# Moving key and value projections and attention heads to other places of a two-layer mixer block

## The reference, cut to what matters

```python
mem_n = rms_norm(mem, mem_norm_g)
for l in range(2):
    h = rms_norm(x, pre_mix_g[l])
    proj = h @ w_in[l]            # lx, ly, fq, fk, fv, ff, rq, rk, rv, rg
    lru_out = rg_lru(conv(lx)) * gelu(ly)                 # recurrence over time
    fox_out = forgetting_attention(fq, fk, fv, ff, b_f)   # 8 heads, causal, forget gate ff
    ret_out = retention(rq, rk, rv, rg, positions)        # 4 heads, rotary, decay
    x = x + rms_norm(concat(lru_out, fox_out, ret_out) @ w_out[l], post_mix_g[l])
    h = rms_norm(x, pre_cross_g[l])
    k, v = mem_n @ w_ck[l], mem_n @ w_cv[l]               # depend on mem only, not on x
    x = x + rms_norm(attend(h @ w_cq[l], k, v) @ w_co[l], post_cross_g[l])
    h = rms_norm(x, pre_ffn_g[l])
    x = x + rms_norm((silu(h @ w_gate[l]) * (h @ w_up[l])) @ w_down[l], post_ffn_g[l])
```

## Time and profile before

| | |
|---|---|
| Median of 3 runs | 2499.45 us (2499.06 to 2500.43) |
| The profiled execution | 2499.28 us, span 2497.5 us |
| PE busy | 1922.5 us (77%), 12804 instructions |
| DVE busy | 812.4 us (33%) |
| ACT busy | 520.6 us (21%) |
| POOL busy | 82.9 us (3%) |
| DMA | 739.81 MB, mean 296 GB/s |

### The profile page before, as it was taken

The page is one execution under the profiler, slowest core; times in us unless marked ns, Lnnn a source line. Parts: engine busy times, 40 slices in busy tenths (PEclk is TensorE's granted clock), DMA queues, the critical chain, the costliest instruction groups (busy, mean ns, idle before and its releaser), DMA issues.

```text
span 2497.5 us, 29128 instructions
## 1 busy us (share of the span) xinstructions
PE 1922.5 (77%) x12804; PEld 1253.0 (50%) x12804; DVE 812.4 (33%) x1271; ACT 520.6 (21%) x776; POOL 82.9 (3%) x140
## 2 busy tenths in 40 slices
PE   8999899979998999788766666666666566665665
PEld 7769799869797999677411221121221122111221
DVE  4545467666454576655301100110001010110012
ACT  5434433335254333333100000000000000000000
POOL 1100000011000000010000000000000000000000
PEclk9869999989799999887788877877877778786887
DMA  8215366744153667534799999999999999999996
GB/s 266 99 59 178 105 205 221 237 156 152 60 179 102 205 224 245 169 102 168 293 429 430 429 429 428 429 429 429 429 429 430 429 428 430 428 431 428 430 428 277
DMA packets 171069, 739.81 MB, mean 296 GB/s; under 512 B 6672, under 2 KB 133136, under 8 KB 146240
## 3 DMA queue, kind: packets, MB, share of 16 engines
q1 hardware_dynamic: 168592, 731.27, 73.5%
q0 software_dynamic: 2352, 6.69, 0.8%
HBM read 736.88 MB, written 1.05 MB: 295 GB/s over the span
## 4 chain that ended last, share of the span: by engine, by line
DMA 50%; PE 33%; DVE 11%; ACT 4%; issue 2%; SPq 0%; POOL 0%; DVEq 0%; ACTq 0%
PE PS L317 32%; DMA WB<-in_w_down 23%; DMA WB<-in_w_up 22%; DMA W<-in_w_down 5%; DVE WL L1354 4%; DVE S L1349 3%; ACT WH L911 2%; DVE X L1349 1%; DVE N L1419 0%; PE PS L499 0%; DMA W<-in_w_in 0%; DVE C L1346 0%; DVE S L1346 0%; DVE T L1346 0%; POOL T L2022 0%
## 5 line engine op out<-in xcount | busy, mean ns | idle before, releaser
L317 PE MATMUL PS<-WB,XS 128*32 128x352 f32 x3072 | 364.9, 637 | 210.6 <-DMA WB<-in_w_up 123.8
L1354 DVE TENSOR_TENSOR WL<-W,WH 128x2048 fp32r<-128x2048 f32 x141 | 325.1, 2305 | 245.7 <-ACT WH L911 245.6
L317 PE MATMUL PS<-WB,S 128*32 128x512 f32 x1408 | 273.5, 769 | 150.4 <-issue 77.7
L317 PEld LDWEIGHTS PS<-WB,XS 128*32 128x32 f32 x3072 | 116.6, 141 | 456.7 <-issue 179.4
L317 PE MATMUL PS<-HTh,WH 128*128 128x256 f32 x1064 | 307.5, 289 | 10.1 <-DVE WL L1354 4.7
L911 ACT ACTIVATE WH<-W 128x2048 fp32r<-128x2048 f32 x141 | 269.0, 1908 | 207.6 <-DMA W<-in_w_down 106.2
L1349 DVE SCALAR_TENSOR_TENSOR S<-S,PS 128x352 f32<-128x352 f32 (+1 forms) x110 | 63.3, 587 | 759.9 <-ACT S L1319 752.6
L317 PE MATMUL PS<-HTl,WH 128*128 128x256 f32 x1064 | 302.9, 285 | 0.0
L317 PE MATMUL PS<-HTh,WL 128*128 128x256 f32 x1064 | 302.7, 284 | 0.0
L317 PEld LDWEIGHTS PS<-WB,S 128*32 128x32 f32 x1408 | 73.3, 128 | 339.8 <-issue 225.4
L317 PEld LDWEIGHTS PS<-HTh,WH 128*128 128x128 f32 x1064 | 205.9, 194 | 12.7 <-DVE WL L1354 5.2
(11 more groups left out here) (262 smaller groups left out, 2188.8 us busy)
## 6 DMA issues: line engine op xcount, KB each, us to landing
WB<-in_w_down SPq DMA_DIRECT2D x64, 2816.0 KB, 36.0
WB<-in_w_gate SPq DMA_DIRECT2D x48, 2816.0 KB, 35.7
WB<-in_w_up SPq DMA_DIRECT2D x48, 2816.0 KB, 35.6
C<-in_w_gate SPq DMA_DIRECT2D x16, 2816.0 KB, 36.1
C<-in_w_up SPq DMA_DIRECT2D x16, 2816.0 KB, 37.3
W<-in_w_in SPq DMA_DIRECT2D x31, 1024.0 KB, 7.5
S<-in_w_ada SPq DMA_DIRECT2D x24, 1024.0 KB, 5.3
W<-in_w_gate SPq DMA_DIRECT2D x22, 1024.0 KB, 10.0
```

What stands on the lines that cost most here:

```text
L317: return e.matmul(o, l, r, start=start, stop=stop, skip_group_check=True)
L1354: e.tensor_tensor(M.WL[i][:, :], M.W[:, 2048 * (m % NW):2048 * (m % NW) + 2048], M.WH[i][:, :].bitcast(F32), ALU.subtract).then_inc(*up("l ...
```

## The change

One table, `FILL`, says where each of the 16 key and value units of both layers goes. In each mixer three of them stand among the heads and the output units; the others stand after the post-norms, by `norm_after`, in three programs (PE's is shown). Layer 1's keys are made after layer 0's cross attention and feed-forward. In the mixer attention heads start after the fifth unit and one stands between each pair of units; the output units of the attention come before that of the recurrence, between retention heads. On DVE a head's maxima come before the next unit's low half and its probabilities after it; on ACT a head's exponents come after the high half. `Beside` gets a second lane, in which the parameters and the memory's norm advance at the same time as the forget gate and the recurrence. In the feed-forward the modulation load comes after the down unit's, and the first one of a layer waits for the mixer's output product and not for the cross attention's. `CV` and `CK` get the columns of `XN` and `GA`, `post_norm` works in the first 2048 columns of `S`, the accumulators `AD` move to free columns of `C1`, and the gate bias is loaded in layer 1's feed-forward. The cross attention's first query unit waits for each part of its input as it needs it.

```diff
+FILL = {("mix", 0): (("k", 0), ("k", 1), ("k", 2)), ("post_mix", 0): (("k", 3), ("v", 0), ("v", 1), ("v", 2), ("v", 3)),
+        ("post_cross", 0): (("k", 0), ("k", 1)), ("post_ffn", 0): (("k", 2), ("k", 3)),
+        ("mix", 1): (("v", 0), ("v", 1), ("v", 2)), ("post_mix", 1): (("v", 3),), ("post_cross", 1): (), ("post_ffn", 1): ()}
...
-        self.jobs = []
-
-    def add(self, *jobs):
-        self.jobs.extend(jobs)
+        self.lanes = [[], []]
+
+    def add(self, *jobs, lane=0):
+        self.lanes[lane].extend(jobs)
 
     def step(self, n=1):
         for _ in range(n):
-            if self.jobs:
-                try:
-                    next(self.jobs[0])
-                except StopIteration:
-                    self.jobs.pop(0)
+            for jobs in self.lanes:
+                if jobs:
+                    try:
+                        next(jobs[0])
+                    except StopIteration:
+                        jobs.pop(0)
 
     def finish(self, job):
-        while job in self.jobs:
+        while any(job in jobs for jobs in self.lanes):
...
-    M.CST = C1[:, 0:NCONST]
+    M.CST, M.AD = C1[:, 0:NCONST], [C1[:, NCONST + 256 * i:NCONST + 256 + 256 * i] for i in range(2)]
...
-    M.CQ, M.CK, M.CV = view(0, 8, 256), view(2048, 8, 256), view(4096, 2, 1024)
+    M.CQ, M.TMP = view(0, 8, 256), view(0, 2, 1024)
+    M.CV, M.CK = M.XN, N1[:, 2048:4096].rearrange("p (a b) -> p a b", a=8)
     M.A = [view(512 * i, 2, 256) for i in range(2)]
-    M.AD = [view(1024 + 256 * i, 256) for i in range(2)]
...
+    def norm_after(place, name, layer):
+        units = FILL[place]
+        nrm = norming(name)
+        next(nrm)
+        if len(units) < 2:
+            for u in units:
+                fill(layer, *u)
+            for _ in nrm:
+                pass
+            return
+        for u in units[:-1]:
+            fill(layer, *u)
+        beside.add(nrm)
+        fill(layer, *units[-1])
+        beside.finish(nrm)
...
+        heads(0)
+        proj_t("w_in", l, 3, HT, ("q", l, 1))
+        heads(1)
+        proj_t("w_in", l, 5, HT, ("kk", l, 1))
+        heads(2)
+        proj_r("w_in", l, 7, HT, ("vv", l, 1))
+        heads(3)
+        proj_r("w_in", l, 8, HT, ("rq", l), off=8)
+        heads(4)
+        proj_r("w_in", l, 9, HT, ("rk", l), off=8)
+        heads(5)
+        proj_r("w_in", l, 10, HT, ("rv", l), off=8)
+        heads(6)
+        proj_r("w_in", l, 11, HT, ("rg", l), off=8)
+        heads(7)
+        if l == 0:
+            beside.finish(memory)
+            e.wait_ge(*free("turn", ("mem",), 6))
+        f0, f1, f2 = FILL[("mix", l)]
+        fill(l, *f0)
+        heads(8)
+        e.wait_ge(*at("rot", l, 1, 1))
+        for w, src in (("tq", M.RQ), ("tk", M.RK)):
+            for _ in turning((w, l), [src[:, 0, :], src[:, 1, :]], 2):
+                pass
+        fill(l, *f1)
+        heads(9)
+        ret_s(0)
+        ret_s(1)
+        y = ("mix", l)
+        e.wait_ge(*free("o", l, 1))
+        out_unit("w_out", l, 1, y, of=None if l == 0 else ("ffn", l - 1), start=True)
+        beside.finish(rec)
+        psY = two(take(("ry", l), hold=True))
+        ret_v(0)
+        ret_v(1)
+        ret_s(2)
+        ret_s(3)
+        e.wait_ge(*free("o", l, 3))
+        out_unit("w_out", l, 2, y)
+        ret_v(2)
+        ret_v(3)
+        drop(("ry", l))
         last = retained()
         beside.add(last)
         e.wait_ge(*at("lru", l))
-        y = ("mix", l)
-        out_unit("w_out", l, 0, y, of=None if l == 0 else ("ffn", l - 1), start=True)
-        e.wait_ge(*free("o", l, 3))
-        out_unit("w_out", l, 1, y)
-        out_unit("w_out", l, 2, y)
+        out_unit("w_out", l, 0, y)
+        fill(l, *f2)
         beside.finish(last)
         e.wait_ge(*free("turn", ("ret", l), 0))
         out_unit("w_out", l, 3, y, last=True)
...
             proj_t("w_up", l, n, HT, ("u", l, n))
-            C.units.order.append(("ada", 12 * l + n))
             if n > 1:
                 down(n - 2)
+            C.units.order.append(("ada", 12 * l + n))
         down(9)
-        C.units.order.append(("ada", 12 * l + 11))
         ada_sum(12 * l + 9)
         down(10)
+        C.units.order.append(("ada", 12 * l + 11))
...
+    pre_norm(("mix", 0))
     for l in range(2):
-        pre_norm(("mix", l))
         mixer(l)
-        e.wait_ge(*free("turn", ("mem",), 6))
-        fill_k(l, 0)
-        nrm = norming(("cross", l))
-        fill_k(l, 1)
-        next(nrm)
-        fill_k(l, 2)
-        beside.add(nrm)
-        fill_k(l, 3)
-        for n in range(4):
-            fill_v(l, n)
-        beside.finish(nrm)
-        e.wait_ge(*free("turn", ("cross", l), 6))
+        norm_after(("post_mix", l), ("cross", l), l)
         cross(l)
-        pre_norm(("ffn", l))
+        norm_after(("post_cross", l), ("ffn", l), 1)
         ffn(l)
+        if l == 0:
+            norm_after(("post_ffn", 0), ("mix", 1), 1)
...
+        unit(heads, 0)
+        q_out(1)
+        unit(heads, 1)
...
         def heads(i):
             if i < 8:
-                scores(i)
+                maxima(i)
+            unit(rest, i)
+        def rest(i):
+            if i < 8:
+                probabilities(i)
...
+        heads(8)
+        heads(9)
+        decayed(0)
+        decayed(1)
+        beside.finish(rec)
+        decayed(2)
+        decayed(3)
...
+        if l:
+            e.wait_ge(*at("y", "cross", 1))
+            for g in range(2):
+                e.dma_start(M.GA[:, g, :], D["b_ada_2"][0:1, 2048 + 3072 * g:3072 + 3072 * g].broadcast_to([128, 1024])).then_inc(
+                    *up("ga", *((0,) if g == 0 else ()), by=16))
...
-        e.wait_ge(*(at("ada_acc", ADA[i - 2]) if i % 12 > 1 else at("y", "cross", i // 12)))
+        e.wait_ge(*(at("ada_acc", ADA[i - 2]) if i % 12 > 1 else at("y", "mix", i // 12)))
```

More of the change, by code:

```diff
@@ L461, in mixer @@
         fg, rec = forget(), recurrence()
-        beside.add(fg)
+        beside.add(fg, rec)
+        memory = norming(("mem",), M.XN, M.D3)
         if l == 0:
[L464 to L470, removed]
+            beside.add(parameters(), memory, lane=1)
+        proj_t("w_in", l, 2, HT, ("q", l, 0))
+        proj_t("w_in", l, 4, HT, ("kk", l, 0))
+        proj_r("w_in", l, 6, HT, ("vv", l, 0))
         beside.finish(fg)
[L472 to L475, removed]
         def scores(h):
@@ L519, in heads @@
                 values(i - 2)
[L521 to L534, removed]
         def ret_s(h):
@@ L922, in early, with unit @@
             high(m)
-    def unit():
+    def unit(between=None, *args):
         nonlocal here
@@ L967, in post_squares, with fill_out, norm_after @@
                     *up("ysq", *y, t, h))
+    def fill_out(l, kind, n):
+        if kind == "k":
+            e.activation(M.CK[:, 2 * n:2 * n + 2, :], two(full("k", l, n)), ACT.Copy).then_inc(*freed("k", l, n))
+        else:
+            e.activation(M.CV[:, :, 256 * n:256 * n + 256], two(full("v", l, n)), ACT.Copy).then_inc(*freed("v", l, n))
+    def norm_after(place, nrm, layer):
+        units = FILL[place]
+        if len(units) < 2:
+            early()
+            next(nrm)
+            for u in units:
+                unit()
+                fill_out(layer, *u)
+            run_all(nrm)
+            return
+        unit()
+        next(nrm)
+        fill_out(layer, *units[0])
+        for u in units[1:-1]:
+            unit()
+            fill_out(layer, *u)
+        beside.add(nrm)
+        unit()
+        fill_out(layer, *units[-1])
+        beside.finish(nrm)
     def parameters():
@@ L1045, in mixer @@
         fg, rec = forget(), recurrence()
-        beside.add(fg)
+        beside.add(fg, rec)
         if l == 0:
[L1048 to L1057, removed]
-        beside.finish(fg)
-        if l == 0:
-            beside.finish(pars)
-        unit()
-        e.activation(M.S1, two(full("rq", l)), ACT.Copy).then_inc(*freed("rq", l))
-        unit()
-        e.activation(M.QR, two(full("rk", l)), ACT.Copy).then_inc(*freed("rk", l))
+            memory = norming(("mem",), par("mem", 0, 8), ("mem",), M.XN, MEM, M.NSQ)
+            beside.add(parameters(), memory, lane=1)
+        unit()
+        q_out(0)
+        unit()
+        k_out(0)
+        unit()
+        v_out(0)
+        beside.finish(fg)
         def scores(h):
@@ L1092, in heads @@
                 values(i - 2)
-        heads(0)
-        unit()
-        e.activation(M.RV, two(full("rv", l)), ACT.Copy).then_inc(*freed("rv", l))
-        heads(1)
-        unit()
-        ps = two(full("rg", l))
-        e.wait_ge(*at("rot", l, 0, 1))
-        e.activation(M.S1, ps, ACT.Tanh, scale=0.5).then_inc(*up("rg_tanh", l))
-        for i in range(2, 10):
-            heads(i)
-            beside.step()
-        beside.finish(rec)
         def retained():
@@ L1457, in ada_sum, with norm_after @@
         stt(o, i, 1.0 if sec in (1, 4) else 0.0, b, ALU.add, ALU.add).then_inc(*freed("ada", n))
+    def norm_after(place, nrm):
+        units = FILL[place]
```

(39 more changed lines are left out.)

173 lines of the change are left out of this document (79 added, 94 removed).

## The result

The changed kernel takes 2477.8 us (2474.7 to 2482.7, 4 runs) against 2499.6 (2499.1 to 2500.4): ratio 0.9914, interval 0.9897 to 0.9931, 22 us faster. The forecast was 76 us faster, and its range, 2406 to 2460, doesn't reach the measured time. The profiled execution took 2478.76 us, its span is 2477.0. The page first: slices of PE and DMA, and the chain that ended last by engine (before: the earlier trace rows). DMA's part of the chain fell from 50% to 46%, PE's rose from 33% to 41%.

A forecast was written before the change was run, and what follows sets the result against it. It took the first block as bound by TensorE and the experts as a weight stream that moves forward one for one. Stage changes summed to -76.2 us from the profiled 2499.28, giving 2423.1 us, with 2406 to 2460 at about 8 in 10.

The forecast's parts named there:

- so the rounds should hide behind PE: Mixers: DVE's and ACT's work per round fits behind PE's 9.4 us of a unit and a head.
- I take 10 and 6: Mixers: all PE waits together, 10 us in layer 0 (bounds 0 and 25), 6 in layer 1 (0 and 15).
- the clock above 0.97: Mixers, first w_in to last w_out product: 163 and 155 us, with TensorE's clock above 0.97.
- my case: The forecast's own case: 2423.1 us, range 2408 to 2440, chance 0.62.
- (2): Rival: mixer rounds late as an in-order DVE or ACT queues a low half behind a waiting step; 35 us, 2458; chance 0.17.
- (1): Rival: the clock falls at each head in the mixers; 16 heads x 2.7 = 43 us, 2466; chance 0.08.
- (3): Rival: in the mixers one chain through DVE and PE stalls PE at each of 16 heads; slower, 2519; chance 0.04.
- (4): Rival: the second half's stream doesn't start earlier, held by something outside the first block; 2499; chance 0.02.
- (5): Rival: all waits vanish, mixers 16 us less and norms 2; 2405; chance 0.07.
- The feed-forwards: Modulation load behind the down unit's: eleven steps at 17.6 us plus waits, -15.3 us in layer 0, -12.0 in layer 1.
- the stages after the mixers and after layer 0's cross attention: Fewer units after the mixers: -17.25 and -39.5 us; two units after layer 0's cross attention: +3.5 us.
- Both stages after the feed-forwards: Layer 0's, with units added, +3.6 us to 20.8; layer 1's +1.2 us, as DVE's chain gains less than PE.

The follow-up runs named there:

- E1: The changed kernel with one edit: PE takes the PSUM bank that has been free longest, not the next in turn; 2437.3 us, ratio 0.9755 to the kernel before.
- E4: The changed kernel, banks still in turn, but the bank a pair of heads has just given up is passed over once; 2448.0 us, ratio 0.9781.
- E7: The changed kernel with banks by longest free, without the forget gate's eight 8-row products in each head's scores; 2410.0 us, ratio 0.9631.
- E3: The kernel before with one edit: in the feed-forward each modulation block is loaded after the down unit's weights; 2480.5 us, ratio 0.9916.
- E5: The kernel before with one edit: PE takes the bank that has been free longest; 2486.8 us, ratio 0.9952.
- E8: The changed kernel with the mixers of before, their key and value units after them, and banks by longest free; 2452.3 us, ratio 0.9807.

## Why the prediction was wrong

**The step that failed** is "so the rounds should hide behind PE", with its term "I take 10 and 6" of waits and the clock above 0.97. I counted what DVE and ACT have to do in a round and found room, and the room is there: nowhere in E1 does PE wait for a low half inside the rounds. What I left out is the resource by which PE is tied to them, four PSUM banks in a fixed turn. A bank of a pair of heads is held for two rounds and released by the last and least urgent operation of the chain; before the change the unit behind it was most often just another head's small product, and one wait of 0.93 us for the same subtraction stood in the trace, for which I gave no row:

```profile
131.65 2.08 PE L317 MATMUL PS<-S,BD 128*128 128x256 f32 x4 [0.93 <-DVE MXl L1648]
```

With units between heads and low halves on DVE between them, the same release came 2.3 to 4.4 us late in three places of each mixer. E4 gives these places 30 us, the whole of E1's edit 40.

The sum had a second term at nothing, the clock: it took the mixers' products at full rate. Of the 49.8 us by which the mixers missed, 21.5 are idle time (37.5 against 16) and 28.3 busy time. With E1's banks the idle time is 14.6, and 12.7 us of clock remain. The 2437.3 us of E1 lie inside the own range of my case (2408 to 2440), but near its upper end, and for that remainder, which the sum didn't have.

**The rivals.** (2), rounds late by a part through a queue in order, had the right shape, but its 2458 is 20 us short; it named the low half as what PE waits for and had no clock in it. (1), at 2466, is 12 short: none of the priced cases gives the measured time. (1), the clock at each head, is partly true: it falls at heads without a wait ahead of them, and no longer does so in layer 1 when their 8-row products are left out (E7), but at some of them, not at each. A wait and a low clock behind it often come together, and I priced the waits alone: E1 removed 23.0 us of idle time and got 15.6 us of clock with it, E4 20.9 and 5.9. (3), (4) and (5) are out; the second block started 17.5 us earlier, the experts 20.7, and these took 1261.0 us, as before (1260.8).

**What held.** The feed-forwards (forecast 196.1 and 198.0, measured 196.3 and 199.0) for the reason given. In layer 0's last step SP now issues the down weights at 488.88 and the modulation behind them (before 508.54), and PE's wait of 6.05 us is gone:

```profile
488.47 0.37 SPq L2218 DMA_DIRECT2D S<-in_w_ada  x1
488.88 1.09 SPq L2212 DMA_DIRECT2D W<-in_w_down  x2
506.71 0.37 SPq L2218 DMA_DIRECT2D S<-in_w_ada  x1
```

Held too: the stages after the mixers and after layer 0's cross attention, to 1.4 us. Both stages after the feed-forwards are longer than forecast, 4.0 and 2.1 us. PE now reaches its end without the old wait, in which DVE used to catch up: its last accumulation runs until 524.4, behind a low half, and PE waits for it before the first unit.

```profile
524.51 1.12 PE L324 MATMUL PS<-C 128*32 128x1 f32 x16 [4.36 <-DVE C L1411]
```

```profile
518.17 2.29 DVE L1416 TENSOR_TENSOR WL<-W,WH 128x2048 fp32r<-128x2048 f32 x1 [1.99 <-ACT WH L941]
...
520.76 3.61 DVE L1411 SCALAR_TENSOR_TENSOR C<-S,T,C 128x256 f32<-128x256 f32 x7
```

**The rule that I argued away.** The prediction set idle gaps, the cause given by the Trainium skill, "TensorE: Matmul & The Clock Gate", section "HAM oscillation — how this bites in real kernels", against a busy window at 0.50, and took the clock as solved once the loops were broken up. In the changed kernel, by short windows, six of the 13 low stretches of the mixers begin in a wait of PE or at its end, as that section has it, and three within 3.3 us behind one. It isn't the whole: the other four begin before a wait or, as at 77 and 131, over 10 us behind the last one. And the same wait of 2.85 us before the same turning has a low clock behind it in layer 0 (196 to 201) and none in layer 1, where it stayed at 1.00, in E7 as in the changed kernel itself:

```profile
713.38 0.66 PE L400 MATMUL PS<-C,S 128*128 128x128 f32 x4 [2.85 <-DVE S L1411]
```

The page "Perfetto Trace Analysis" of the Trainium skill, section "Matmuls", asks that independent groups of products rotate through different PSUM banks so that ACT and DVE can empty one meanwhile. The kernel did rotate; what E1 and E4 add is that a fixed turn isn't enough where one bank is held longer than the others.

**Open.** Why the loop of heads ran at either clock with the same products. And why the second block gains some 3 us (191.9 to 188.7; E3 has 188.7 too): nearly all of it lies in two stretches with the same instructions at a higher clock, 16.3 us at 0.81 from 1108.7 on before, 15.1 at 0.84 from 1091.0 on after, and 8.9 us at 0.50 from 1193.4 on before, 7.4 at 0.61 from 1174.7 on after. What raised the clock there is not known.

## What to carry to other kernels

When work is set between other work, count the buffers that both take in turn, and ask of each what releases it and what now stands in front of that release; engine time per round says nothing of it. Take the buffer that has been free longest: it was worth 40 us in the changed kernel. And a wait of PE is priced with the low clock that may come behind it: two edits that removed 23.0 and 20.9 us of waits took 15.6 and 5.9 us of busy time with them, so from a quarter to two thirds of the wait again. Before a window's clock is taken as the cost of its products, look at the same products in another run.

## What the runs showed of the hardware

- TensorE's clock fell at heads with no wait ahead of them while these had products of 8 rows: layer 1's mixer was at 0.96 with the products (E1) and at 1.00 without (E7), in the same order of work and with the same waits, in one profiled execution each.
- A loop of attention heads, PE busy throughout, was at 1.00 in a window of 10 us in one kernel (E5) and at 0.50 in windows of 20 us in two others (before, E8), with the same products. Seven runs of E5 spread from 2478 to 2499 us, ten of the kernel before from 2485 to 2508.
- DVE's low half (128x2048) took 2.82 us at 116.25, where POOL was busy for 2.92 of 3 us, and 2.29 at the earlier trace rows. Whether POOL is the cause isn't shown.
